# Opening by groups: group 1's mixer half in the gather loop, and the second layer's chains spread over 7/5 as many tiles

## The reference, cut to what matters

```python
q = (xc @ wq).reshape(T, PEER_HEADS, 2, PEER_HALF)
s_top, i_top = lax.top_k(einsum('thpd,pkd->thpk', q, subkeys), 16)
best_s, pos = lax.top_k(cand_s, 16)         # 16 x 16 sums of the two halves
idx = take_along_axis(cand_i, pos)          # 16 experts of 16384, per token and head
act = gelu(einsum('thkd,td->thk', take(u, idx), xc))
y = einsum('thk,thkd->td', softmax(best_s) * act, take(v, idx))
```

## Time and profile before

| | |
|---|---|
| time, median of three | 1787.74 us |
| profiled execution: time, span | 1785.12 us, 1783.0 us |
| PE, DVE, ACT, POOL busy | 86%, 58%, 21%, 60% |
| moved | 682.92 MB, 383 GB/s in the mean |
| first u gather, first v gather | 206.25 us, 228.16 us |
| granted clock, mean | 0.973 |

### The profile page before, as it was taken

One profiled execution on the slowest core, in us unless ns is written; L12 is line 12 of the kernel. 1 busy time (PEld: TensorE's weight loads), 2 busy tenths in 40 slices (PEclk: granted clock), 3 DMA queues, 4 the chain that ended last, 5 costly groups with the idle time before them and its releaser, 6 DMA issues.

```text
span 1783.0 us, 13512 instructions
## 1 busy us (share of the span) xinstructions
PE 1524.6 (86%) x3952; PEld 662.9 (37%) x3952; DVE 1029.9 (58%) x2479; ACT 381.8 (21%) x959; POOL 1068.3 (60%) x1131
## 2 busy tenths in 40 slices
PE   4997949999898878999997777999999777777777
PEld 3754424443232323444442223444443222222223
DVE  6547772686665653255377774336449885444542
ACT  2121222221111122142121113133222212111110
POOL 4212366767565674446467775447547777777773
PEclk9998969999999999999999998999999999999999
DMA  9997479999999999999999999999999999999996
GB/s 374 399 367 256 148 274 404 398 405 404 405 405 405 407 409 384 383 375 404 402 405 409 409 409 406 367 390 409 402 361 406 409 408 405 409 410 409 410 409 270
DMA packets 212573, 682.92 MB, mean 383 GB/s; under 512 B 20851, under 2 KB 21525, under 8 KB 212502
## 3 DMA queue, kind: packets, MB, share of 16 engines
q0 software_dynamic: 158976, 578.88, 82.6%
q1 hardware_dynamic: 52464, 101.79, 15.3%
q10 hardware_dynamic: 1062, 1.40, 0.2%
HBM read 680.94 MB, written 1.05 MB: 383 GB/s over the span
## 4 chain that ended last, share of the span: by engine, by line
PE 42%; DMA 29%; POOL 17%; issue 6%; DVE 5%; ACT 1%; POOLq 0%; DVEq 0%
PE pair L990 19%; PE pair L181 15%; DMA net_u<-in_peer_u,net_cols 11%; DMA net_v<-in_peer_v,net_cols 10%; POOL net_v L564 8%; POOL net_u L564 8%; DMA net_w<-in_b_w_qo 2%; DMA net_w<-in_peer_wq 2%; DVE net_u L1748 2%; PE pair L194 2%; PE pair L201 1%; DMA net_v<-in_ada_w 1%; DMA net_w<-in_kv_w 1%; PE pair L592 1%; PE pair L731 1%
## 5 line engine op out<-in xcount | busy, mean ns | idle before, releaser
L990 PE MATMUL pair<-net_v,net_diags 128*128 128x512 f32 x2048 | 977.2, 611 | 158.3 <-DMA net_v<-in_peer_v,net_cols 158.0
L564 POOL DMA_INDIRECT net_v<-in_peer_v,net_cols x512 | 500.8, 978 | 338.2 <-PE pair L990 216.1
L990 PEld LDWEIGHTS pair<-net_v,net_diags 128*128 128x128 f32 x2048 | 367.1, 191 | 715.9 <-DMA net_v<-in_peer_v,net_cols 362.3
L564 POOL DMA_INDIRECT net_u<-in_peer_u,net_cols x512 | 505.2, 987 | 210.7 <-issue 133.0
L1748 DVE SCALAR_TENSOR_TENSOR net_u<-net_u,pair 128x1024 f32<-128x1024 f32 x384 | 464.1, 1217 | 254.7 <-DMA net_u<-in_peer_u,net_cols 254.3
L181 PE MATMUL pair<-net_w,net_work 128*128 128x512 f32 x640 | 300.8, 616 | 37.7 <-DMA net_w<-in_b_w_qo 16.3
L1332 ACT ACTIVATE net_diags<-ident,net_cols 128x128 f32<-128x128 f32 x512 | 170.9, 390 | 685.1 <-DVE net_cols L1428 685.1
L1748 DVE SCALAR_TENSOR_TENSOR net_u<-net_u,net_x_tok 128x1024 f32<-128x1024 f32 x128 | 156.3, 1222 | 110.8 <-DMA net_u<-in_peer_u,net_cols 110.4
L181 PEld LDWEIGHTS pair<-net_w,net_work 128*128 128x128 f32 x640 | 124.4, 198 | 189.8 <-issue 173.0
L223 POOL DMA_DIRECT2D net_u<-in_ada_w x46 | 24.8, 543 | 80.9 <-DVE net_cols L235 20.1
L1428 DVE TENSOR_TENSOR net_cols<-net_cols,net_gate 128x4 f32<-128x4 f32 (+1 forms) x124 | 19.7, 159 | 92.0 <-ACT net_cols L1325 91.9
(11 more groups left out here) (242 smaller groups left out, 958.9 us busy)
## 6 DMA issues: line engine op xcount, KB each, us to landing
net_w<-in_peer_wq SPq DMA_DIRECT2D x12, 2048.0 KB, 19.8
net_u<-in_ada_w POOLq DMA_DIRECT2D x46, 512.0 KB, 8.3
...
net_v<-in_ada_w POOLq DMA_DIRECT2D x18, 512.0 KB, 12.7
net_u<-in_kv_ada_w POOLq DMA_DIRECT2D x16, 512.0 KB, 4.8
net_u<-in_peer_u,net_cols POOLq DMA_INDIRECT x512, 11.5
```

The lines of the kernel that those rows point to most:

```text
L564: eng.indirect_dma_start(slot, None, rows, bass.IndirectOffsetOnAxis(ap=idx[:, i, k:k + 1], axis=0)).then_inc(landed, 16)
L990: mm = eng.matmul(acc[q % 2][:, at], diag[n % DIAGS][:, :], vb[n % V_SLOTS][:, at], start=(k == 0), stop=(k == SEL - 1))
```

## The change

Group 1's v1, o0, o1 and out blocks go behind group 0's whole mixer, and sums, root, y and residual of group 1 go into the first tiles of the gather loop. o0 and out0 are loaded once more for group 1, as `o0b` and `out0b`, in slot 1. The slices go round in another order, the last one is loaded behind u tile 3, and its sum is awaited there. The u gathers of tiles 4 and later come after that wait; `out1` of group 1 is still awaited before v tile 0. Queries 2 to 7 start at 12 instead of 1, rows and vectors later. In `chain` every offset t is `slower(t)`, t * 7 // 5, on all engines, save WQ_EVERY. The diff, cut (in the chains only the first and last of the offsets are shown; ACT's and DVE's are changed alike):

```diff
     EDGES = list(range(0, PER, 2 * BATCH)) + list(range(PER, N + 1, BATCH))
-    NEAR_AT = 32
+    NEAR_AT = 48
...
             ph.sb("w1", [P, 4 * D])[:, :])]
+        o_cols = 2 * qk_cols + v_cols
+        wo = a["a_w_out"][0]
...
                   "v0": (wi, 2 * qk_cols, GROUP, 2), "v1": (wi, 2 * qk_cols + WCOLS, GROUP, 3),
-                  "o0": (wi, 2 * qk_cols + v_cols, GROUP, 4), "o1": (wi, 2 * qk_cols + v_cols + WCOLS, GROUP, 0),
-                  "out0": (a["a_w_out"][0], 0, GROUP, 1), "out1": (a["a_w_out"][0], WCOLS, GROUP, 2)}
-        wide = [f"wq{n}" for n in range(4)] + [f"vec{n}" for n in range(8)]
-        for n in range(4):
-            blocks[f"wq{n}"] = (a["peer_wq"][0], n * WCOLS, GROUP, 3 + n % 2)
+                  "o0": (wi, o_cols, GROUP, 4), "o1": (wi, o_cols + WCOLS, GROUP, 0),
+                  "out0": (wo, 0, GROUP, 1), "out1": (wo, WCOLS, GROUP, 2),
+                  "wq0": (a["peer_wq"][0], 0, GROUP, 4), "o0b": (wi, o_cols, GROUP, 1),
+                  "wq1": (a["peer_wq"][0], WCOLS, GROUP, 3), "out0b": (wo, 0, GROUP, 1)}
+        wide = ["wq2", "wq3"] + [f"vec{n}" for n in range(8)]
+        for n in range(2, 4):
+            blocks[f"wq{n}"] = (a["peer_wq"][0], n * WCOLS, GROUP, 4 - n % 2)
...
-        order = [("k", 0), ("k", 1), ("q", 0), ("q", 1), ("v0", 0), ("v0", 1), ("v1", 0), ("v1", 1),
-                 ("o0", 0), ("o1", 0), ("out0", 0), ("out1", 0), ("o0", 1), ("wq0", 0), ("o1", 1), ("wq1", 0),
-                 ("out0", 1), ("out1", 1)] + [(f"wq{j}", g) for g, j in FIRST[2:]]
+        order = [("k", 0), ("k", 1), ("q", 0), ("q", 1), ("v0", 0), ("v0", 1), ("v1", 0), ("o0", 0), ("o1", 0),
+                 ("out0", 0), ("out1", 0), ("wq0", 0), ("v1", 1), ("o1", 1), ("wq1", 0), ("o0b", 1), ("out0b", 1),
+                 ("out1", 1)] + [(f"wq{j}", g) for g, j in FIRST[2:]]
...
-                     ada_slots, [n if n < 16 else (4, 5, 6, 7, 16, 17)[(n - 16) % 6] if n < 48 else 4 + n % 4
+                     ada_slots, [n if n < 16 else (4, 5, 6, 7, 16, 17)[(n - 16) % 6] if n < 48 else (6, 7, 4, 5)[n % 4]
...
-        QUERY_AT = {2: 1, 3: 3, 4: 6, 5: 12, 6: 18, 7: 24}
-        ROW_AT, VEC_AT, VEC_EVERY = 34, 40, 9
+        QUERY_AT = {2: 12, 3: 14, 4: 17, 5: 22, 6: 27, 7: 32}
+        ROW_AT, VEC_AT, VEC_EVERY = 46, 52, 8
         VEC_END = VEC_AT + VEC_EVERY * (VECTORS - 1) + 3
+        def slower(tiles):
+            return tiles * 7 // 5
+
...
+        def query_bank(r):
+            return bank[3] if r == 1 else bank[6 + r % 2]
...
-            for name in ("v0", "v1", "o0", "o1", "out0", "out1"):
+            for name in ("v0", "v1", "o0", "o1", "out0", "out1", "wq0"):
...
             eng.dma_start(wf[:, :, :], wk.rearrange("(c p) n -> p c n", p=P)[:, :, 2 * D:2 * D + FX_H]
                           ).then_inc(f_in, 16)
-            for name in wide:
+            for name in ["o0b", "wq1", "out0b"] + wide:
...
-            ada.load(eng, 16, 38)
+            ada.load(eng, 16, 37)
             mlstm_root(0)
-            ada.load(eng, 54, 22)
+            ada.load(eng, 53, 15)
             norm_root(2)
-            ada.load(eng, 76, 4)
-            mlstm_root(1)
+            ada.load(eng, 68, 11)
 
             def roots():
-                yield 4 - 13
+                yield 12 - POOL_SHIFT
+                mlstm_root(1)
+                yield 26 - POOL_SHIFT
                 norm_root(3)
...
-            eng.wait_ge(ada.added, ADA)
...
                     if n >= U_SLOTS:
                         eng.wait_ge(dot_done, n - U_SLOTS + 1)
+                    if n == 4:
+                        ada.load(eng, ADA - 1, 1)
+                        eng.wait_ge(ada.added, ADA)
                     behind.upto(n)
...
-            eng.wait_ge(ml_evac, 1)
-            pj.whole(eng, "v1", 1, bank[4], Dw)
...
             key_scores(0, bank[5], (bank[0],))
-            eng.wait_ge(ml_evac, 6)
+            pj.whole(eng, "o0", 0, bank[1], C)
+            eng.wait_ge(ml_evac, 7)
+            eng.wait_ge(arg_done, 1)
+            sums(0, pair[2])
+            pj.whole(eng, "o1", 0, bank[6], C)
             eng.wait_ge(ada.added, 4 * DC)
             eng.wait_ge(gate_in, 16)
             for half in range(2):
@@ -683,36 +698,27 @@
                 mm = eng.matmul(pair[1][:, half * 512:(half + 1) * 512], chip.ones[0:1, :],
                                 gate_bias[:, half * 512:(half + 1) * 512], start=False, stop=True)
             mm.then_inc(row_ps, 1)
+            eng.wait_ge(y_ready, 1)
+            turn(pair[2], A).then_inc(ml_turned, 1)
+            eng.wait_ge(so_done0, 2)
+            key_scores(1, bank[0], (bank[1], bank[6]))
+            eng.wait_ge(row_copied, 1)
+            eng.wait_ge(ml_yT, 1)
+            pj.whole(eng, "out0", 0, bank[2], E)
+            pj.whole(eng, "out1", 0, bank[3], E)
             eng.wait_ge(cols_done, 2)
             column_sums(cols, DC, DC, AUX[:, 2 * DC:3 * DC])
-            pj.whole(eng, "o0", 0, bank[1], C)
-            eng.wait_ge(ml_evac, 8)
-            eng.wait_ge(arg_done, 1)
-            sums(0, pair[2])
-            pj.whole(eng, "o1", 0, bank[6], C)
-            eng.wait_ge(row_copied, 1)
-            eng.wait_ge(so_done0, 1)
-            key_scores(1, bank[0], (bank[1], bank[2]))
-            eng.wait_ge(y_ready, 1)
-            turn(pair[2], A).then_inc(ml_turned, 1)
             eng.wait_ge(ada.added, 5 * DC)
             column_sums(sc0, 0, DC, AUX[:, 3 * DC:4 * DC])
-            eng.wait_ge(ml_yT, 1)
             eng.wait_ge(sd_done, 3)
-            pj.whole(eng, "out0", 0, bank[2], E)
-            pj.whole(eng, "out1", 0, bank[3], E)
-            eng.wait_ge(pw_done, 3)
-            sums(1, pair[0])
-            eng.wait_ge(x_mix, 1)
-            pj.part(eng, "o0", 1, bank[2], Dw, 0)
+            pj.part(eng, "v1", 1, bank[0], Dw, 0)
             eng.wait_ge(xs_done, 3)
             turn(pair[2], A).then_inc(x_turned, 1)
-            pj.part(eng, "o0", 1, bank[2], Dw, 1)
 
...
-            pj.whole(eng, "o1", 1, bank[3], Dw)
+            pj.part(eng, "v1", 1, bank[0], Dw, 1)
             eng.wait_ge(sc_done, 1)
             turn_tokens(0, 0)
-            eng.wait_ge(hmean, 2)
+            pj.whole(eng, "o1", 1, bank[2], Dw)
             query(1, "wq1", C, 0)
             query(1, "wq1", C, 1)
             eng.wait_ge(copied, 1)
             turn_query(1)
+            eng.wait_ge(pw_done, 3)
+            eng.wait_ge(ml_evac, 8)
+            sums(1, pair[0])
+            score_keys(1)
+            pj.whole(eng, "o0b", 1, bank[3], Dw)
             eng.wait_ge(y_ready, 2)
             turn(pair[0], B).then_inc(ml_turned, 1)
-            score_keys(1)
-            eng.wait_ge(ml_yT, 2)
-            eng.wait_ge(so_done0, 4)
-            pj.whole(eng, "out0", 1, bank[2], F)
-            pj.whole(eng, "out1", 1, bank[3], F)
             eng.wait_ge(sc_done, 2)
             eng.wait_ge(ada.added, 6 * DC)
             column_sums(sc0, DC, DC, bank[5][:, 0:DC])
-            eng.wait_ge(xs_done, 4)
-            turn(pair[1], B).then_inc(x_turned, 1)
+            eng.wait_ge(ml_yT, 2)
+            eng.wait_ge(so_done0, 4)
+            pj.whole(eng, "out0b", 1, bank[2], F)
+            pj.whole(eng, "out1", 1, bank[3], F)
 
             def first_queries():
                 for r in range(2, 8):
                     g, j = FIRST[r]
+                    if r == 2:
+                        yield QUERY_AT[2] - 3
+                        eng.wait_ge(xs_done, 4)
+                        turn(pair[1], B).then_inc(x_turned, 1)
                     yield QUERY_AT[r]
...
-                s, e = START[g], START[g] + END[g]
+                s, e = START[g], START[g] + slower(END[g])
...
-                yield s + 6
+                yield s + slower(6)
...
-                yield s + 8
+                yield s + slower(8)
...
-                    yield e + 13 + 5 * WQ_EVERY
+                    yield e + slower(13) + 5 * WQ_EVERY
...
-            eng.wait_ge(row_ps, 1)
-            eng.activation(row_mix[:, :], pair[1][:, :], ACT.Copy).then_inc(row_copied, 1)
...
+            eng.wait_ge(row_ps, 1)
+            eng.activation(row_mix[:, :], pair[1][:, :], ACT.Copy).then_inc(row_copied, 1)
...
+            eng.wait_ge(ml_rows, 2)
+            for h in range(ML_H):
+                done = eng.activation(pw[1][:, h * P:(h + 1) * P], bank[0][:, h * P:(h + 1) * P], ACT.Exp,
+                                      bias=acol[:, 0, h:h + 1], scale=-1.0)
+            done.then_inc(pw_done, 1)
...
-            head_squares(1, pair[0])
-            eng.wait_ge(pj.done, pj.through("o0", 1))
-            eng.activation(so[1][:, 0:WCOLS], bank[2][:, :], ACT.Sigmoid).then_inc(so_done0, 1)
...
+            take_values("v1", 1, WCOLS, bank[0])
+            copy_tokens(0, 0)
             eng.wait_ge(pj.done, pj.through("o1", 1))
-            eng.activation(so[1][:, WCOLS:2 * WCOLS], bank[3][:, :], ACT.Sigmoid).then_inc(so_done0, 1)
-            copy_tokens(0, 0)
```

(62 more changed lines are left out.)

169 lines of the change are left out of this document (83 added, 86 removed).

## The result

| | before | after |
|---|---|---|
| time, median | 1787.74 us (1785.43 to 1791.03) | 1800.7 us (1796.97 to 1803.3) |
| profiled execution: time, span | 1785.12, 1783.0 us | 1802.24, 1800.4 us |
| first u gather, v tile 0, u tile 13 | 206.25, 228.16, 240.30 us | 185.14, 239.40, 240.65 us |

The ratio is 1.007, with a 95% interval of [1.0053, 1.0086]: the change costs 13 us where 11 were forecast to be won, outside the range. This is on a chip where the kernel before takes some 1788 us.

A forecast was written before the change was run, and what follows sets the result against it. Bound by bytes, so only idle transfer time could be won: 1785.1 - 1.9 (opening) - 8.5 (chains) = 1774.7 us, 1777 on the median's level. Range 1762 to 1794.

The forecast's parts named there:

- Opening: Start to paired gather stream: first gather 22 us earlier, u 13 at 238.5, net gain 1.9 us, bounds -14 to +13.
- rivals 1, 2 and 5: Opening: 1, quick restart, 1766 (0.18); 2, out1 gates the stream, 1798 (0.14); 5, TensorE at 1.2 GHz, 1789 (0.05).
- Chains: Second layer's chains of groups 2 and 3: spreading blocks to 7/5 gains 8.5 us, bounds nothing to 18.7.
- The third of the dip at 1320: Stage at 1320 us: a third of its 4.8 us idle transfer time given back, part of the 8.5 us.
- Rival 3: Chains: the spread gives nothing, idle time only moves, opening as forecast; 1786 us, chance 0.11.
- I put 0 there, up to 5 us if it is longer: Query stage: POOL's stop while route(2) waits for scores, 7.66 us in the kernel before, costs 0, up to 5.
- The 287 for xn_done: Gather loop, TensorE tile 12: after waiting for xn_done behind DVE tile 26, TensorE goes on at 287 us.
- still run back to back: Gather loop: queries of r = 2 to 7 follow one another, five tiles and 16.8 us each, tile 42 ending at 388.
- v slots come free no later: Gather loop: TensorE tile 42 ends at 388 against about 391 before, so v slots are not delayed.
- The later end is covered: End of the chains: route(12) in DVE tiles 362 to 379, POOL needs its index at 377; two tiles late cost nothing.
- Rival 4: Gather loop: queries, blocked twice, starve v slots; 5 us on top of the forecast, 1782 us, chance 0.07.
- changes only DVE's source, 1.22 us either way: Near-token copy at tile 48: only where DVE reads the tokens changes, 1.22 us either way, no cost put down.

The follow-up runs named there:

- e2: Kernel before with only the two chains' offsets spread to 7/5 (READY alike): 1781.1 us, 0.9959 of the kernel before.
- e3: Changed kernel with the chains put back, slower(t) = t: 1803.19 us, 1.0078 of the kernel before.
- e1: Changed kernel with NEAR_AT 32 instead of 48: 1792.69 us, 1.0014 of the kernel before.
- e13: Changed kernel with group 1's norm and second query batch earlier, and tokens read from SBUF for 24 tiles in the last group: 1783.25 us, 0.9979 of the kernel before.
- e15: Changed kernel with group 1's mod, norm and second query batch earlier, tokens from SBUF for 48 tiles as there: 1786.58 us, 0.9992 of the kernel before.

## Why the prediction was wrong

**Opening: right but for 3 us.** First u gather 185.14 for 184.1, tile 0 of DVE at 197.97 for 196.8, the stop for load 79 (landed 6.3 us after its issue for 5), v 0 at 239.40 for 237.2 behind out1, and 15.70 us for the two blocks against 16.3; rivals 1, 2 and 5 are out. The terms written for the end of o0b add up to 203.1 us, not 204.5; it was 206.1. u 13 left at 240.65 for 238.5, no sooner than the 240.30 of before. By windows 9.4 us of idle time went in 0 to 240 against 10.3 of bytes: 0.9 us lost, forecast 1.9 us gained.

**Chains: right in size.** 8.9 us of idle time gone in 660 to 1440 for the 8.5 written; 404 and 396 GB/s against 382 and 385, waits of POOL for v slots 36.5 us for 58.3. The third of the dip at 1320 did not come, it moved, and the other two gave more. e2, the spread alone, has 0.9959 or 7.3 us. Rival 3 is out for the kernel before; in the changed kernel the gain of the stage shows and that of the time does not (e3). "The later end is covered" held.

**The step that failed: the query stage, "I put 0 there, up to 5 us if it is longer".** The 287 for xn_done was right (288.03). Wrong was what followed. The six queries "still run back to back", so tile 42 would end at 388, against 391 in before, and "v slots come free no later": TensorE stood 9.17 us inside query 2 and ended tile 42 at 400.3, against 392.9, so v slots came later. And the 7.66 us stop of before had been free because gathers landed 15.4 us after their issue then; the stop of 8.37 us in after found 6.4 to 7.5. The stage cost 14.7 us of idle time, three times the upper bound, 9.0 of them in 340 to 360 us. Rival 4 had the mechanism, with 5 us and a chance of 0.07; its price was what was wrong.

**The second: the last loop, put at nothing by "changes only DVE's source, 1.22 us either way".** True for DVE (1222 ns in the mean, by the page's row), wrong for POOL: in 1440 to 1580 us 25 of 101 issues took more than 1.05 us, up to 1.98, against 8 of 108 in before, and nothing but issues paces the transfers there. It cost 10.3 us of the profile. The 48 tiles are the smaller part of it: with 32 (e1) 7.2 of the 10.6 us stay, so most came with the phase into which the opening's half of the change brought the two engines, and why is open. By the times, the tiles beyond 24 or 32 cost between 2 us (e13 against e15, by their ratios) and 8 (e1 against after).

So of the 10.4 us forecast from opening and chains 8.0 came in (-0.9 and 8.9); the two stages costed at nothing took 25.
